# Routing logits for four row tiles at once, and the last multiplication split over three engines

## What is computed

```python
def rmsnorm(x, g):
    xf = x.astype(jnp.float32)
    y = xf * lax.rsqrt(jnp.mean(xf * xf, axis=-1, keepdims=True) + EPS)
    return (y * g.astype(jnp.float32)).astype(x.dtype)

def moe_ffn(xt, rg_w, rg_b, re_w, re_b, w13, w2):      # xt = rmsnorm(hl) * (1 + scale) + shift
    g_prob = jax.nn.softmax((xt @ rg_w + rg_b), axis=-1)
    g_w, g_idx = lax.top_k(g_prob, 1)
    e_logits = (xt @ re_w + re_b).reshape(T, N_GROUPS, EXP_PER_GROUP)
    ...                                                # top 2 of the chosen group's 8, then the experts
hl = hl + g2 * moe_ffn(...)
return rmsnorm(hl, final_g)
```

## Time and profile before

| what | value |
|---|---|
| time, median of 3 runs | 2263.57 us (2260.22 to 2264.07) |
| the profiled execution's own time | 2262.39 us |
| its span | 2260.6 us |
| TensorE busy | 2022.6 us, 89% |
| VectorE busy | 789.4 us, 35% |
| ScalarE busy | 365.9 us, 16% |
| GpSimd busy | 238.0 us, 11% |

### The profile page before, as it was taken

One profiled execution on the slowest core, in us unless ns is written; L12 is line 12 of the kernel. 1 busy time (PEld: TensorE's weight loads), 2 busy tenths in 40 slices (PEclk: granted clock), 3 DMA queues, 4 the chain that ended last, 5 costly groups with the idle time before them and its releaser, 6 DMA issues. The chain is left out here.

```text
span 2260.6 us, 20875 instructions
## 1 busy us (share of the span) xinstructions
PE 2022.6 (89%) x7648; PEld 907.6 (40%) x7648; DVE 789.4 (35%) x1581; ACT 365.9 (16%) x778; POOL 238.0 (11%) x523
## 2 busy tenths in 40 slices
PE   5999999999999969997889859999996999888882
PEld 2555444444443444442333224444554444333330
DVE  3778311235333752221111124464734222111113
ACT  2111212212203121111111112110002111111111
POOL 1000000000000012221222100000000222222120
PEclk9999999999999969999999989999996999999996
DMA  9898522220103589999999961221352999999994
GB/s 363 296 368 318 206 70 87 105 102 34 65 0 114 192 343 423 421 421 422 422 422 423 416 240 59 68 84 35 122 213 99 418 423 420 422 423 422 422 413 162
DMA packets 121191, 592.09 MB, mean 262 GB/s; under 512 B 25704, under 2 KB 43872, under 8 KB 80489
## 3 DMA queue, kind: packets, MB, share of 16 engines
q1 hardware_dynamic: 94494, 548.03, 60.2%
q10 hardware_dynamic: 14412, 25.59, 3.1%
q0 software_dynamic: 12160, 16.83, 2.0%
HBM read 571.13 MB, written 42.31 MB: 271 GB/s over the span
## 5 line engine op out<-in xcount | busy, mean ns | idle before, releaser
L542 PE MATMUL bank<-w,xT 128*64 128x512 f32 x1920 | 433.1, 597 | 45.2 <-DMA w<-in_moe_w 37.3
L562 PE MATMUL bank<-w,hT 128*64 128x512 f32 x1168 | 277.4, 617 | 48.3 <-DMA w<-in_moe_w 40.7
L542 PEld LDWEIGHTS bank<-w,xT 128*64 128x64 f32 x1920 | 154.1, 138 | 310.0 <-issue 258.0
L734 DVE COPY hT<-bank 128x256 f32<-128x256 f32 x73 | 30.9, 424 | 512.9 <-PE bank L550 512.9
L1139 PE MATMUL bank<-uhi,wnh 128*128 128x512 f32 x384 | 168.4, 593 | 0.9 <-ACT uhi L888 0.9
L562 PEld LDWEIGHTS bank<-w,hT 128*64 128x64 f32 x1168 | 89.4, 141 | 185.6 <-issue 138.9
L493 ACT ACTIVATE oh<-bank 128x256 f32<-128x256 f32 x73 | 28.0, 383 | 785.0 <-PE bank L542 785.0
L1535 PE MATMUL bank<-uT,wo 128*128 128x512 f32 x256 | 133.8, 604 | 3.8 <-DVE uT L1421 3.8
L739 DVE TENSOR_TENSOR ohs<-bank,g2h 128x512 f32<-128x512 f32 x73 | 50.5, 691 | 234.6 <-PE bank L562 234.6
L1139 PEld LDWEIGHTS bank<-uhi,wnh 128*128 128x128 f32 x384 | 71.8, 190 | 86.9 <-issue 85.8
L542 PE MATMUL bank<-w13x,xT 128*64 128x512 f32 x416 | 94.4, 593 | 8.0 <-DMA w13x<-in_moe_w 8.0
(11 more groups left out here) (436 smaller groups left out, 2133.1 us busy)
## 6 DMA issues: line engine op xcount, KB each, us to landing
w<-in_moe_w SPq DMA_DIRECT2D x177, 2048.0 KB, 34.7
adab<-in_ada_w SPq DMA_DIRECT2D x24, 2048.0 KB, 11.5
w13x<-in_moe_w SPq DMA_DIRECT2D x18, 2048.0 KB, 34.1
wnh<-in_h_in_w SPq DMA_DIRECT2D x12, 1024.0 KB, 5.2
wo<-in_m_in_w SPq DMA_DIRECT2D x4, 2048.0 KB, 17.9
wo<-in_m_in_w ACTq DMA_DIRECT2D x4, 2048.0 KB, 17.6
ow<-in_m_out_w SPq DMA_DIRECT2D x8, 1024.0 KB, 6.8
d_xm<-xmb ACTq DMA_DIRECT2D x16, 385.5 KB, 5.9
```

The lines of the kernel that those rows point to most:

```text
L542: ins = t_.matmul(b[n * C:(n + 1) * C, :].rearrange("c (g f) -> c g f", g=2), xT[:, k, half * C:(half + 1) * C], w13s[i][:, k, n], start=( ...
L562: ins = t_.matmul(b_y[m * C:(m + 1) * C, :], hT[:, k, half * C:(half + 1) * C], w2[:, u, kk, m * 512:(m + 1) * 512], start=(kk == 0), stop ...
```

## The change

Two separate edits.

1. In `expert_ffn`, the logits of the four row tiles are formed together: one VectorE multiplication of all 4 x 36 products by the row factors (broadcast along the 36) into a new tile `lall`, then one addition of `cst` for the group logits and one for the expert logits. Eight instructions become three.
2. In the last stage the multiplication by `fg` and by the row factors is shared. For row tiles 1 and 3 GpSimd multiplies `hl` by `fg` into a new tile `gained`, which lies where expert weights were, and ScalarE then scales that by the row factors. VectorE keeps row tiles 0 and 2. The stores are issued in the order 1, 0, 3, 2.

```diff
-                w13x = T("w13x", [P, KH, 2 * DE]); vt = w13x; cst = T("cst", [P, NR])
+                w13x = T("w13x", [P, KH, 2 * DE]); vt = w13x; cst = T("cst", [P, 1, NR]); lall = T("lall", [P, TL, NR])
...
-                    own(v.tensor_tensor(cst[:], lgb[:, TL * NR:(TL + 1) * NR], rb[:], ALU.add))
-                    for t in range(TL):
-                        lg = lgb[:, t * NR:(t + 1) * NR]
-                        v.scalar_tensor_tensor(out=LG[:, t, :], in0=lg[:, 0:NGRP], scalar=rss[:, t:t + 1], in1=cst[:, 0:NGRP], op0=ALU.mult, op1=ALU.add)
-                        own(v.scalar_tensor_tensor(out=LE[:, t, :], in0=lg[:, NGRP:NR], scalar=rss[:, t:t + 1], in1=cst[:, NGRP:NR], op0=ALU.mult, op1=ALU.add))
+                    own(v.tensor_tensor(cst[:].rearrange("p o n -> p (o n)"), lgb[:, TL * NR:(TL + 1) * NR], rb[:], ALU.add))
+                    own(v.tensor_tensor(lall[:], lgb[:, 0:TL * NR].rearrange("p (t n) -> p t n", t=TL), rss[:].rearrange("p (t o) -> p t o", o=1).to_broadcast([P, TL, NR]), ALU.mult))
+                    v.tensor_tensor(LG[:], lall[:, :, 0:NGRP], cst[:, :, 0:NGRP].to_broadcast([P, TL, NGRP]), ALU.add)
+                    own(v.tensor_tensor(LE[:], lall[:, :, NGRP:NR], cst[:, :, NGRP:NR].to_broadcast([P, TL, NE]), ALU.add))
...
+            gained = put("gainedf", [P, TL // 2, D], W13)
...
             @blk.sync
-                for t in range(TL):
-                    sp.wait_ge(s_of, t + 1)
-                    sp.dma_start(out[0, t * P:(t + 1) * P, :], hl[:, t, :]).then_inc(s_out, 16)
+                for i in range(TL // 2):
+                    sp.wait_ge(s_oa, i + 1)
+                    sp.dma_start(out[0, (2 * i + 1) * P:(2 * i + 2) * P, :], gained[:, i, :]).then_inc(s_out, 16)
+                    sp.wait_ge(s_of, i + 1)
+                    sp.dma_start(out[0, 2 * i * P:(2 * i + 1) * P, :], hl[:, 2 * i, :]).then_inc(s_out, 16)
...
             @blk.scalar
+                act.wait_ge(s_nf, 1)
+                for i in range(TL // 2):
+                    act.wait_ge(s_gn, i + 1)
+                    nc.scalar.activation(gained[:, i, :], gained[:, i, :], ACT.Copy, scale=ss[:, 2 * i + 1:2 * i + 2]).then_inc(s_oa, 1)
+
+            @blk.gpsimd
+            def _(pool):
+                pool.wait_ge(s_fg, 16)
+                for i in range(TL // 2):
+                    pool.wait_ge(s_hlf, 2 * i + 2)
+                    nc.gpsimd.tensor_tensor(gained[:, i, :], hl[:, 2 * i + 1, :], fg[:], ALU.mult).then_inc(s_gn, 1)
...
             @blk.vector
                 rsqrt(v, own, r1[:], ss[:], r2[:])
+                v.memset(r1[:, 0:1], 0.0).then_inc(s_nf, 1)
                 dve.wait_ge(s_fg, 16)
-                for t in range(TL):
+                for t in range(0, TL, 2):
                     v.scalar_tensor_tensor(out=hl[:, t, :], in0=hl[:, t, :], scalar=ss[:, t:t + 1], in1=fg[:], op0=ALU.mult, op1=ALU.mult).then_inc(s_of, 1)
```

More of the change, by code:

```diff
@@ L2306, in build @@
         with stage() as c:
-            fg = sbt(c, "fg", [P, D]); junk = sbt(c, "junkf", [P, D])
+            fg = sbt(c, "fg", [P, D]); junk = sbt(c, "junkf", [P, D]); gained = put("gainedf", [P, TL // 2, D], W13)
             yg = [sbt(c, f"ygf{t}", [P, 2, D])[:] for t in range(TL)]
@@ L2310, in build @@
             ss = sbt(c, "ssz", [P, TL]); r1 = sbt(c, "r1z", [P, TL]); r2 = sbt(c, "r2z", [P, TL])
-            s_fg = sem("s_fg"); s_sqf = sem("s_sqf"); s_df = sem("s_df"); s_of = sem("s_of"); s_out = sem("s_out")
+            s_fg = sem("s_fg"); s_sqf = sem("s_sqf"); s_df = sem("s_df"); s_of = sem("s_of"); s_out = sem("s_out"); s_gn = sem("s_gn"); s_nf = sem("s_nf"); s_oa = sem("s_oa")
             blk = c.enter_context(nc.Block())
```

## The result

| | median | lowest to highest | runs |
|---|---|---|---|
| before | 2261.18 us | 2259.14 to 2264.76 | 14 |
| changed | 2266.07 us | 2262.19 to 2267.11 | 14 |

The ratio is 1.0017, 95% interval 1.0009 to 1.0025: some 2 to 6 us slower. I had forecast 2262.7, no measurable change, with "GpSimd holds VectorE up" as the rival at 0.35. Its size stays under the 0.2% that I had set, but the interval excludes both no change and the gain of 0.9 us that the forecast's sum gave.

A forecast was written before the change was run, and what follows sets the result against it. DMA engines streaming expert weights, and the stores at the end, were taken as the bound. 0.83 (layer 1) + 0 (layer 0) + 0.07 = 0.9 us gave 2261.5, or 2262.7 against the median; range 2259.8 to 2267.4.

The forecast's parts named there:

- GpSimd holds VectorE up: Last stage: GpSimd's products delay VectorE's second sum of tile 3 and its factors, 2.65 us at d = 2.0; chance 0.35.
- what covers them is the rest of VectorE's sums and the twelve tiny instructions: Last stage: GpSimd's two products, taken at 2.0 us each, are hidden beside VectorE's work and end before or as ScalarE needs them.
- rival A: Last stage: GpSimd's products hold VectorE up ahead of the first store, giving 2265.4 us, or 2265.9; chance 0.35.
- 2d - 1.35: Last stage: price of GpSimd holding VectorE up, d being one GpSimd product's duration; 2.65 us at d = 2.0.
- estimate of 2.25 for d: Last stage: one GpSimd product's duration, half of 4.497 us for 2048 elements; it would give 2265.9 us.
- gains nothing: Layer 0's expert stage: the earlier gather lands at the same time behind the weight loads; 0 taken, bounds 0 to 0.75 us.
- Their start does not depend on VectorE: Layer 0: the weight loads ahead of the gather are started by ScalarE's copies and stores; gain taken as 0.
- Edit 1's price: Logits: three instructions of about 0.31, 0.17 and 0.29 replace eight; with the wait for GpSimd's tables, 0.75 us gained in layer 0.
- layer 1's gain: Layer 1's expert stage: gather and weight stream start earlier with the logits, the whole 0.83 us counted.
- Only the first store's issue counts: Last stage: four stores fill the DMA engines, so faster tiles only queue; first store 0.07 us earlier, gain 0.07, not 2.4.

The follow-up runs named there:

- edit1_only: The new logits in both layers with the last stage as before, against the kernel before: ratio 1.0002 (0.9993 to 1.0011).
- later_gather_l0: The kernel before with five tiny VectorE instructions added in layer 0 to issue the first gather later: issue at 17.71, transposes at 21.43, layer 0's stage 531.4 us.
- half_first_store: The kernel before with row tile 0's product formed and stored in two halves of 512 columns: ratio 0.9992 (0.9983 to 1.0001).
- warm_tensor: The kernel before with needless TensorE matmuls while it waits for the first gather and behind the transposes: ratio 0.9996 (0.9985 to 1.0007).
- edit2_only: The old logits with the whole last-stage change, against the kernel before: ratio 1.0018 (1.0009 to 1.0028), last stage 30.8 us.

## Why the prediction was wrong

- **The step that failed** is "what covers them is the rest of VectorE's sums and the twelve tiny instructions". The GpSimd products were priced at nothing because they lie beside other work; that work was held up by them. It cost 2.96 us in the profile, 30.75 against 27.79, and the same in three executions (30.75, 30.81, 30.80). I had the mechanism and the place as rival A and gave it 0.35. Its price 2d - 1.35 gives 3.3 with the measured d of 2.34; the runs showed 1.96 + 1.06, since the product is recorded from 0.4 us before the gap and finished 0.14 earlier than a start at the gap plus d. That the changed kernel's 2266.07 lies near A's 2265.4 and 2265.9 is in part luck: A meant 1.8 to 2.3 us over the kernel before, and the medians differ by 4.9. What I weighed wrongly was the evidence: one tiny instruction at 0.338 beside a gather looks like the same exclusion (it ended at 1741.20, the gather at 1741.23; no run isolates it), and I set it off against an instance that had not collided. The estimate of 2.25 for d, worked out from the page "GPSIMD Engine Reference" of the Trainium skill (the side-by-side accounting, whose figure is for an addition), was good: 2.34 measured.
- **Layer 0 "gains nothing"**: the reason was half right (the gather lands when the weight loads ahead of it have ended), the value was not. "Their start does not depend on VectorE" holds, but their end does: with the gathers issued 0.7 earlier it came at 21.2 to 21.6 instead of 20.5 to 21.0. So the gather landed 0.5 to 0.8 later, and TensorE's clock rose too late for the first product. The five executions with the new logits in both layers and no added matmul had the late load and stages of 534.1 to 536.3, against 531 to 532 in most others. The early-late difference is 3.1 us (534.8 - 531.6), the load and the dip together. Two of the six kernels with the old logits and neither delay nor added matmuls in layer 0 had it too, so it is a matter of odds. The times leave open how much of it the change costs on average: edit1_only is at 1.0002, and -0.76 + 3.1 would be 1.0010, near its upper end.
- **Edit 1's price and layer 1's gain** were right: three instructions of 0.31, 0.17 and 0.28, the wait for the last table, and transposes 0.76 earlier against 0.83. Layer 1's stage is 508.6 long on average in the eleven profiles with the new logits and 509.2 in the eight with the old ones, so about 0.6 of it reached the end. Once (later_gather_l0, layer 1 untouched) the transposes were 0.7 late with nothing changed.
- **"Only the first store's issue counts"**: right in the changed kernel, where the offload of two products brought nothing, wrong as a rule (half_first_store).
- **The sum with what was measured**: +2.96 (last stage) - 0.76 (layer 1) + 3.1 (layer 0, where the kernel before has the early load) = +5.3; against a kernel before that itself has the late load, +2.2. The measured interval is 2.0 to 5.7 us. The two profiled executions themselves differ by 3.9: +3.0 in the last stage, +5.3 in layer 0's, -0.9 in layer 1's, -3.1 in the stage between them and -0.4 before, of which the last two lie where no edit is.

Open: why the weight loads end later when the gathers are issued earlier, and in warm_tensor with the old issue; and whether the late load brings the dip about. The scatter that hides these effects in single times goes with the granted clock too. The stage between the two expert layers is 385.8 us long in five of the nineteen profiled executions and 388.9 in the others, with old and new logits alike: the clock falls 7.4 to 7.9 us before its end in the five and 14.6 to 15.4 before it in the fourteen. From 15 to 7.5 us before its end, in the kernel before (388.9) and in the changed one (385.8):

```profile
1708.42:1715.92 7.50, 7.50 (x40) 7.50 (x38) 0.69 (x1) 1.63 (x3) 0.00 (x0) 0.51 0.01 2
```
```profile
1710.22:1717.72 7.50, 6.30 (x57) 6.33 (x58) 1.74 (x3) 1.64 (x3) 0.00 (x0) 1.00 0.01 2
```

And layer 0's expert stage begins at 798.3 to 799.1 in the eight executions in which the clock stays at 2.4 GHz until then, and at 802.8 to 804.0 in the eleven in which it has fallen 8.9 to 10.3 us before. Each of these steps is as large as the effects studied here.

## What to carry to other kernels

Work given to GpSimd beside a busy VectorE is not free because it is off the path: each long GpSimd instruction that reads SBUF can hold a VectorE instruction until it ends, and the held instruction shows as a long one, not as a wait. Before making producers faster, look at whether the transfers behind them are full. And shifts of less than a microsecond ahead of a stage should be judged by where its first loads and the clock's rise land, over several profiled executions, not by their sum.

## What the runs showed of the hardware that was not expected

- A one-input `tensor_scalar` on 128x4 elements was held for 1.16 and 0.71 us by GpSimd memsets (1.33 and 0.88 recorded), while a 128x1024 two-input instruction beside such a memset kept its 1.28, and a `tensor_scalar` on 128x1 its 0.15.
- GpSimd's 128x1024 product takes 2.34 us, a 128x1024 memset 0.94 to 0.97.
- 0.01 us in the start of TensorE's transposes (21.51 in before, 21.52 in edit2_only) went with a first product of 5.01 or 6.65 us, by the moment at which the granted clock rose (28.0 or 31.3 us into the stage). One execution at 21.55 had the short one (5.33), so it is an edge and not a fixed limit.
- The packets of two gathers (0.38 MB), the first issued at 16.1 to 17.7 us with 4 MB of weight loads under way, did not move before 19.6 to 20.2, though in layer 1, with nothing ahead of it, the first packet started 1.64 us after the issue. The earlier issue made the weight loads end later (21.2 to 21.6 against 20.5 to 21.0), and the gather landed 0.6 to 0.85 after them each time.
- Stages that no edit touched differ by 3.1 and 4.7 us from one execution to the next, each time with the granted clock high or low in their last 7 to 10 us.
